# Both feed-forward stages of a two-layer decoder by one level of Strassen

## The reference

```python
def rmsnorm(x, g):
    y = xf * lax.rsqrt(jnp.mean(xf * xf, axis=-1, keepdims=True) + EPS)
    return (y * g.astype(jnp.float32)).astype(x.dtype)

def conv_ffn(h, prev, w_up, conv_w, conv_b, w_down):
    l = h.shape[1]
    u = h @ w_up                                   # 1024 -> 2 * 2816
    ext = jnp.concatenate([prev, u], axis=1)
    y = conv_b + sum(conv_w[k] * ext[:, k:k + l] for k in range(CONV_WIDTH))
    a, v = jnp.split(y, 2, axis=-1)
    return (jax.nn.silu(a) * v) @ w_down, ext[:, -(CONV_WIDTH - 1):]
```

## Time and profile before

| | |
|---|---|
| median of 3 runs | 3037.19 us (3033.56 to 3038.42) |
| span of the profiled execution | 3038.0 us |
| PE busy | 2935.1 us, 97% of the span |
| PEld busy | 2715.8 us, 89% |
| DVE busy | 1574.7 us, 52% |
| POOL busy | 966.5 us, 32% |
| ACT busy | 815.3 us, 27% |
| granted clock of TensorE | 9 tenths of full or more in 38 of the 40 slices of the span |

### The profile page before, as it was taken

The page is one execution under the profiler, slowest core; times in us unless marked ns, Lnnn a source line. Parts: engine busy times, 40 slices in busy tenths (PEclk is TensorE's granted clock), DMA queues, the critical chain, the costliest instruction groups (busy, mean ns, idle before and its releaser), DMA issues. The chain is left out here.

```text
span 3038.0 us, 50987 instructions
## 1 busy us (share of the span) xinstructions
PE 2935.1 (97%) x19316; PEld 2715.8 (89%) x19316; DVE 1574.7 (52%) x3486; ACT 815.3 (27%) x1506; POOL 966.5 (32%) x422
## 2 busy tenths in 40 slices
PE   8998989999989999999999999999999999999998
PEld 7996966666767799999999999997999999999998
DVE  6212158888545418744625535495257626436262
ACT  5002037777623304311201111205133202112020
POOL 4430000000000244544444443460435444444443
PEclk9999989999979999999999999999999999999999
DMA  6116740000457311111111111312111111111112
GB/s 186 54 42 227 252 163 2 2 2 2 149 153 228 128 36 60 40 44 49 38 45 49 34 53 37 129 41 115 43 53 42 40 50 45 40 47 41 50 36 91
DMA packets 128683, 222.76 MB, mean 73 GB/s; under 512 B 16118, under 2 KB 92252, under 8 KB 127344
## 3 DMA queue, kind: packets, MB, share of 16 engines
q1 hardware_dynamic: 108548, 201.57, 20.5%
q10 hardware_dynamic: 19980, 19.14, 2.4%
HBM read 202.61 MB, written 22.18 MB: 74 GB/s over the span
## 5 line engine op out<-in xcount | busy, mean ns | idle before, releaser
L382 POOL TENSOR_SCALAR weights_high<-weights_whole 128x1024 fp32r<-128x1024 f32 (+2 forms) x168 | 434.8, 2588 | 1045.8 <-PE banks L417 878.9
L413 PE MATMUL banks<-ffn_in_high,weights_high 128*128 128x364 f32 (+1 forms) x2112 | 467.0, 329 | 9.6 <-DVE ffn_in_low L280 9.6
L415 PE MATMUL banks<-ffn_in_low,weights_high 128*128 128x364 f32 (+1 forms) x2112 | 466.7, 329 | 0.0
L417 PE MATMUL banks<-ffn_in_high,weights_low 128*128 128x364 f32 (+1 forms) x2112 | 465.2, 329 | 0.0
L384 POOL TENSOR_TENSOR weights_low<-weights_whole,weights_high 128x1024 fp32r<-128x1024 f32 (+2 forms) x168 | 375.7, 2236 | 24.7 <-issue 0.2
L2776 DVE SCALAR_TENSOR_TENSOR conv_out<-conv_ext,conv_w,conv_out 128x1024 f32<-128x1024 f32 x176 | 318.7, 1811 | 114.1 <-ACT conv_out L2708 99.7
L413 PEld LDWEIGHTS banks<-ffn_in_high,weights_high 128*128 128x128 f32 x2112 | 366.1, 189 | 11.4 <-issue 11.4
L417 PEld LDWEIGHTS banks<-ffn_in_high,weights_low 128*128 128x128 f32 x2112 | 367.4, 188 | 0.0
L415 PEld LDWEIGHTS banks<-ffn_in_low,weights_high 128*128 128x128 f32 x2112 | 366.9, 189 | 0.0
L2807 DVE TENSOR_TENSOR x<-x,banks 128x728 f32 (+1 forms) x128 | 86.5, 718 | 385.2 <-PE banks L417 385.2
L2708 ACT ACTIVATE conv_out<-conv_ext,conv_b,conv_w 128x1024 f32<-128x1024 f32 (+1 forms) x176 | 138.3, 835 | 536.1 <-DVEq L2767 536.0
(11 more groups left out here) (433 smaller groups left out, 4616.7 us busy)
## 6 DMA issues: line engine op xcount, KB each, us to landing
weights_whole<-in_w_up SPq DMA_DIRECT2D x88, 512.0 KB, 3.5
past_rows<-in_kv_pages SPq DMA_DIRECT2D x160, 128.0 KB, 2.4
z<-in_kv_pages SPq DMA_DIRECT2D x96, 128.0 KB, 2.4
weights_whole<-in_w_down SPq DMA_DIRECT2D x32, 384.0 KB, 3.1
weights_whole<-in_w_down SPq DMA_DIRECT2D x32, 320.0 KB, 2.9
x<-in_cmp_pages ACTq DMA_DIRECT2D x64, 128.0 KB, 5.8
x<-in_cmp_pages SPq DMA_DIRECT2D x64, 128.0 KB, 5.7
cmp_rows<-in_cmp_pages ACTq DMA_DIRECT2D x64, 128.0 KB, 5.7
```

Of the source, the lines that this page charges most:

```text
L382: pool.tensor_scalar(high, whole, 1.0, None, ALU.mult)
L413: pe.matmul(o, wh, high[:, at], start=kk == 0, stop=False)
L415: pe.matmul(o, wh, low[:, at], start=False, stop=False)
L417: last = pe.matmul(o, wl, high[:, at], start=False, stop=kk == len(terms) - 1)
```

## The change

`conv_ffn` is replaced by `feed_forward`. It works in units. In the up half a unit is one hidden chunk (its a tile and its v tile, 22 units), in the down half two output tiles over a part of the hidden chunks (6 parts, PAIRS, of which five hold 4 chunks and one holds 2; 4 units each). In a unit the weights are a 2 x 2 matrix of blocks (two output tiles by two halves of the input chunks), and the tokens another (two halves of the input chunks by two halves of 544 tokens, TH). The Winograd form of Strassen's scheme gets the four result blocks from 7 block products, where eight were done, with sums of blocks ahead of the products and of products behind them. A block product is 4 input chunks (2 or 1 in the down half) x 3 products x 2 cuts of 272 columns.

- **Weights.** POOL makes the four sums of weight blocks (L2804 to L2812) and the seven low parts (L2797), ACT the seven high parts, in a ring of four blocks; SP loads quarters of weights into six places.
- **Tokens.** They are normalised before the first product: squares (ACT and DVE), sums over the partitions by 72 matmuls of one column (L2845), root (ACT), reciprocal (DVE), a diagonal matrix (L3015) that four matmuls spread over the partitions (L2851). DVE and POOL multiply by it, and make the four sums of token blocks and their seven low parts.
- **Between the halves.** The gated tiles (L3094) go to DRAM (`store`), and come back part by part (`stage`), where ACT cuts the high parts, and DVE the low ones (L3099) and the four sums (L3038).
- **Results.** In the up half ACT copies four blocks of banks per unit and DVE adds three (L3064); in the down half DVE adds each of the 7 products of a unit to `x` (L3112). A product may start when the one two places ahead of it has been read out of its banks.
- The convolution's tiles keep their operations, but the norm is gone from them. `project` no longer cuts the first weights of the stage that follows.

```diff
-PARTS = (6, 6, 5, 5)
+TH = TE // 2
+HP = TH // 2
+KH = KC // 2
+BLOCKS = 7
+RING = 4
+QUARTERS = 6
+PAIRS = (2, 2, 2, 2, 2, 1)
-def conv_ffn(k, layer, w, xn, x, following=(), result=None, saved=None):
...
+def feed_forward(k, layer, w, x, space, following=(), next_w=None, result=None, saved=None):
...
+        LAST_BLOCK = (2, 5, 4, 6)
+        BLOCK_PIECE = (0, 1, 0, None, 2, 1, 3)
...
+            def stage(p):
+                if p == 0:
+                    sp.wait_ge(multiplied, BLOCKS * (FC - 1) + 1)
+                    sp.wait_ge(gated_stored, 16 * 4)
+                elif p == 1:
+                    sp.wait_ge(gated_stored, 16 * FC)
+                else:
+                    sp.wait_ge(d_split, BLOCKS * p)
+                n, at = PAIRS[p], starts[p]
+                for half, dst in enumerate(staged[min(p, 1)]):
+                    src = g_dram[at + half * n:at + (half + 1) * n].rearrange("k p t -> p k t")
+            for q in range(1, UNITS):
+                for piece in range(4):
+                    i = 4 * q + piece
+                    if i >= QUARTERS:
+                        q0, p0 = (i - QUARTERS) // 4, (i - QUARTERS) % 4
+                        sp.wait_ge(w_split, BLOCKS * q0 + LAST_BLOCK[p0] + 1)
+                    sp.dma_start(quarter(q, piece), source(q, piece)).then_inc(q_loaded[i % QUARTERS], 16)
+                    if q == FC and piece == 2:
+                        stage(0)
+                if q == FC + 2:
+                    sp.dma_start(k.outs["conv"][layer], tails[:]).then_inc(stored, 16)
+                    stage(1)
+                elif q > FC + 2 and (q - FC) % PER == 0 and part_of(q) + 1 < len(PAIRS):
+                    stage(part_of(q) + 1)
...
+            def lower(q, j):
+                high, low = ring(q, j)
+                pool.wait_ge(w_rounded, BLOCKS * q + j + 1)
+                pool.tensor_tensor(low, block_source(q, j), high.bitcast(F32), ALU.subtract).then_inc(w_split, 1)
+            def sums(q):
+                a11, a12, a21, a22 = (quarter(q, piece) for piece in range(4))
+                s1 = total[:, 0:width(q) * P]
+                wait_quarter(pool, q, 2)
+                wait_quarter(pool, q, 3)
+                pool.tensor_tensor(s1, a21, a22, ALU.add).then_inc(w_summed, 1)
+                lower(q, 0)
+                lower(q, 1)
+                pool.drain()
+                pool.tensor_tensor(a21, a11, a21, ALU.subtract).then_inc(w_summed, 1)
+                pool.drain()
+                pool.tensor_tensor(a11, s1, a11, ALU.subtract).then_inc(w_summed, 1)
+                pool.drain()
+                pool.tensor_tensor(a12, a12, a11, ALU.subtract).then_inc(w_summed, 1)
+            for q in range(UNITS):
+                sums(q)
+                lower(q, 2)
+                lower(q, 3)
+                if q == 0:
+                    pool.wait_ge(gained, KH)
+                    pool.wait_ge(rstd_ready, 1)
+                    n12 = first_half[:, :, TH:TE]
+                    pool.tensor_tensor(n12, n12, over_half(rstd[:, TH:TE]), ALU.mult).then_inc(pool_normed, 1)
+                    high, low = up_block(4)
+                    pool.wait_ge(rounded, len(UP_ORDER))
+                    pool.tensor_tensor(low, up_quadrant(4), high.bitcast(F32), ALU.subtract).then_inc(last_split, 1)
...
+                src = sq_low[:, kk, :] if kk < 6 else sq_high[:, kk - 6, :]
+                for t in range(NTT):
+                    rows = min(P, TE - t * P)
+                    last = pe.matmul(k.ps[0:rows, 3, t:t + 1], src[:, t * P:t * P + rows], ones[:, 0:1],
+                                     start=n == 0 and t == 0, stop=n == KC - 1, skip_group_check=True)
+            last.then_inc(summed, 1)
+            pe.wait_ge(inverted, 1)
+            flat = spread[:, :, :].rearrange("p a n -> p (a n)")
+            for x_ in range(4):
+                last = pe.matmul(k.ps[:, 4 + x_, 0:HP], ones, flat[:, x_ * HP:(x_ + 1) * HP], start=True, stop=True)
+            last.then_inc(spreaded, 1)
+            def product(q, j):
+                n = width(q)
+                pe.wait_ge(w_split, BLOCKS * q + j + 1)
+                which = "ABAEAEA"[j]
+                wait_read(pe, *((q - 2, "C12"), (q - 1, "C21"), (q, "V1"), (q - 1, "C11"), (q, "V2"), (q, "V5"), (q, "C22"))[j])
+                if q == 0:
+                    if j == 4:
+                        pe.wait_ge(last_split, 1)
+                    elif j:
+                        pe.wait_ge(split, UP_ORDER.index(j) + 1)
+                elif q >= FC and (q - FC) % PER == 0:
+                    pe.wait_ge(d_split, BLOCKS * part_of(q) + DOWN_ORDER.index(j) + 1)
+                wh, wl = ring(q, j)
+                high, low = up_block(j) if q < FC else down_block(part_of(q), j)
+                out = bank(q, which)
...
+                    at = slice(kk * P, (kk + 1) * P)
+                    for z, (a, b) in enumerate(((wh, high), (wh, low), (wl, high))):
+                        for piece in range(2):
+                            last = pe.matmul(out[:, piece, :], a[:, at], b[:, kk, piece * HP:(piece + 1) * HP],
+                                             start=first and kk == 0 and z == 0, stop=kk == n - 1 and z == 2,
...
+                if n >= RING:
+                    act.wait_ge(multiplied, n - RING + 1)
+                if j in (0, 1, 6):
+                    wait_quarter(act, q, BLOCK_PIECE[j])
+                else:
+                    act.wait_ge(w_summed, 4 * q + {3: 1, 4: 2, 2: 3, 5: 4}[j])
+                act.activation(ring(q, j)[0], block_source(q, j), ACT.Copy).then_inc(w_rounded, 1)
...
+            for j, after in ((1, 2), (5, 3), (2, 6), (6, 7), (3, 7), (4, 7)):
+                act.wait_ge(made, after)
+                if j in (3, 4):
+                    act.wait_ge(split, UP_ORDER.index(6) + 1)
+                act.activation(up_block(j)[0], up_quadrant(j), ACT.Copy).then_inc(rounded, 1)
...
+                        last_quadrant(q)
+                    round_weights(BLOCKS * q + j + RING)
+                    if j == 0 and q:
+                        silu(q - 1)
+                    elif j == 2 and q:
+                        store(q - 1)
+                    elif j == 5:
+                        tap(q, 0)
+                    elif j == 6:
+                        tap(q, 1)
+                    if q == FC - 1:
+                        if j == 4:
+                            for block_ in (0, 1, 5):
+                                round_gated(0, block_)
+                        elif j == 6:
+                            for block_ in (2, 3, 4, 6):
+                                round_gated(0, block_)
+                    if p == 0 and i == 7:
+                        silu(FC - 1)
+                    if p == 0 and i == 13:
+                        store(FC - 1)
+                    if p + 1 < len(PAIRS):
+                        for block_, at in zip(DOWN_ORDER, (19, 20, 21, 24, 25, 26, 27) if p == 0 else (8, 9, 10, 15, 16, 17, 18)):
+                            if i == at:
...
+            norm(0)
+            norm(1)
+            lower(0)
+            norm(5)
+            lower(1)
+            dve.wait_ge(pool_normed, 1)
+            difference(n11, n12, n11, made)
+            difference(n12, n22, n12, made)
+            lower(5)
+            difference(n22, n22, n11, made)
+            difference(n21, n21, n22, made)
+            for j in (2, 6, 3):
+                lower(j)
+            dve.wait_ge(last_split, 1)
...
+                tile, half, which = ((0, 0, "A"), (0, 0, "B"), (0, 1, "A"), (1, 1, "E"), (1, 1, "A"), (0, 1, "E"), (1, 0, "A"))[j]
...
+                dve.tensor_tensor(xv, xv, bank(q, which), ALU.add).then_inc(x_added, 1)
+            for q in range(FC):
+                place(q, "C11")
+                place(q, "C22")
+                if q == FC - 1:
+                    lower_gated(0, 0)
+                    lower_gated(0, 1)
+                place(q, "C12")
+                if q == FC - 1:
+                    lower_gated(0, 5)
+                    for j in (3, 4, 2, 6):
+                        gated_sum(0, j)
+                    edges(q, 0)
+                    edges(q, 1)
+                else:
+                    for av in range(2):
+                        edges(q, av)
+                        convolve(q, av, 1)
+                        convolve(q, av, 0)
+                    gate(q)
+            for p in range(len(PAIRS)):
+                for i in range(PER * BLOCKS):
+                    if p == 0 and i in (2, 3, 4, 6):
+                        lower_gated(0, i)
+                    add(FC + p * PER + i // BLOCKS, i % BLOCKS)
+                    if p == 0 and i in (3, 5, 7, 9):
+                        convolve(FC - 1, i // 7, 1 if i in (3, 7) else 0)
+                    if p == 0 and i == 11:
+                        gate(FC - 1)
+                    if p + 1 < len(PAIRS):
+                        late = p == 0
```

(9 more changed lines are left out.)

525 lines of the change are left out of this document (319 added, 206 removed).

## The result

The changed kernel takes 3188.1 us (3186.9 to 3189.8, four runs) against 3036.9, a ratio of 1.0504 [1.0489, 1.0519]: slower by 151 us, where I forecast 75. The profiled execution spans 3187.8 us against 3038.0, 149.8 more; the second stage takes 873.5 of it (2305.52 to 3179.05), 75.3 more than before, the first 69.0 more. The rest is 5.4 us between the stages, 2.0 behind the last, and 1.8 gained ahead of the first.

The account below looks back on a forecast made before the run. It took TensorE's matmul count times spacing as the bound. Matmuls -92.3, start +49, up half +6, between halves +24, staging +20, later parts +29, ends +2 made +37.7 us a stage, +75 in both: 3112 us, range 3010 to 3215.

Parts of the forecast that it names:

- Matmuls: TensorE, both halves: 5544 matmuls of 272 columns at 125.5 ns, 92.3 us less in each stage.
- Rivals 3 and 4: Skill's matmul rule holds at 272 columns, 3004 us, chance 0.04; weight loads bound matmuls at 150 ns, 3384 us, 0.01.
- 72 one-column products ... so they end at some 18 us: Stage start: the sums of squares end at 18 us and the norm at 25, within a start term of +49 us.
- Up half: +6 us: Up half: VectorE and GpSimd taking turns cost 0.3 us for each of 21 units, bounds 0 and 44 us.
- Rival 2: Up half: VectorE's and GpSimd's turns bound it, 23.2 us a unit, 3188 us in all; chance 0.2.
- Rival 1: Turns cost nothing and VectorE is never late at additions: 2987 us, or 3010 at half effect; chance 0.21.
- Turns: VectorE operations on SBUF alone and GpSimd tensor-tensor operations take turns; VectorE operations with an operand in the banks do not.
- Between the halves: +24: Between up and down half: TensorE waits for VectorE's queued work and GpSimd's turns, +24 us a stage, from below 17.
- Staging +20: First down part: fetching gated tiles back from DRAM and VectorE's preparing operations cost +20 us a stage.
- later parts +29: Later down parts: VectorE's additions and preparing operations in one queue cost +29 us a stage, from below 19.
- Ends: +2 a stage: Stage end: next projection's weights cut only after the last unit, last two output tiles leave together, +2 us.
- three signs of being wrong: Up unit over 22.5 us, no down-half gaps at VectorE's additions, or convolution operations beside GpSimd staying at 1.3 us.

Follow-up runs that it names:

- e2: Changed kernel with ScalarE making the up half's last tap before the weight rounding that waits for GpSimd's third sum: 3166.5 us.
- e9: Changed kernel with the tap as in e2, a result addition put before the gate, and ScalarE's store issued after the copy of V5: 3144.8 us.
- e4: Changed kernel with GpSimd's weight sums and low parts cut to 128 columns from each stage's second unit on (work left out): 3102.3 us.
- e5: Changed kernel with the start's sums of squares made by 32 products with a matrix of ones, replacing one-column products and diagonal: 3146.0 us.
- e3: Changed kernel with VectorE making low parts for down products 3, 4 and 6 one addition earlier between the halves: 3158.1 us.
- e7: As e3, with the preparation of the next down part spread out among VectorE's additions: 3153.9 us.
- e11: Changed kernel with e5's start, e9's up half, and eight plain block products per down unit in place of seven: 3003.9 us.

## Why the prediction was wrong in size

- **Matmuls: right.** 125.4 ns from the rows at 256 and 363 columns. The rule columns / 2.4 + 2.5 (the Trainium skill, TensorE: Matmul & The Clock Gate, Back-to-back issue gap), which that section gives for a matmul by itself and not for a stream with weight loads, would be 115.8; the trace differs. Rivals 3 and 4 are out.
- **"72 one-column products ... so they end at some 18 us": the step that failed at the start.** 144 records were taken at 0.129 us, from a row at full clock. In the changed kernel they ran at 0.50 and 0.211 us, 12 us more, the four products with ones took the 4 us of half clock and not 2, and all that follows waits for them: the norm came at 39 us, not 25. The row of before at 18.17 us showed the price at half clock. The chain behind the norm was sized rightly (45 us); but product 2 started only at 79.6 us, behind the copy of V1, so the fifth product came 3 us after that chain's end. Together +16 of 40 us a stage.
- **"Up half: +6 us": mis-sized, +20.** I weighed the engines' loads against the unit (12.6 + 14.3 us) and laid out VectorE alone. What ran over was a chain through ScalarE's queue: GpSimd's third sum, a rounding, the tap, the convolution, the gate, the store, the copy of V5, product 5. e2 takes the first wait out and e9 the last; the load of GpSimd and VectorE is the same there. Rival 2 gave 3188 us, the time that was measured, by luck, and is out all the same: its unit of 23.2 us was 22.0, and is 21.05 in e9 with the same load. Rival 1 is out too: the losses were there in every term, and with less of GpSimd's work beside VectorE 86 us of them go (e4), though how much of that is turns alone no run tells.
- **Turns: right, with one reading off.** The operation of the earlier trace rows at 2709.47 us ends 1.08 us after GpSimd's (2712.52 and 2711.44), not 1.28. In e2 and e5 VectorE's operation ends 1.15 and 2.3 us after GpSimd's, again a little under its own length (1.29 and 2.42).
- **Between the halves: +24, measured 29.** Right in size, but for another reason: 12 us are TensorE and VectorE waiting for each other in turns (e3), not VectorE's amount of work. The wait before the third down product was 7.8 us, not 12.
- **Staging +20 right, later parts +29 four short** (20.4 and 33.3). That VectorE's additions and preparing operations share one queue was the reason given; the rows of e7 and the run e4 add GpSimd's sums, for which ScalarE's queue waits. Plain products need no sums and less of every engine, and have no holes (e11).
- **Ends: +2 a stage, measured 7.4 in both.** The first product of the next projection waits 9.6 us for its low part.

The sum fell short by 40 us a stage: 16 start, 14 up half, 5 between, 4 later parts. All four had the right sign, and each was taken in the lower half of its own bounds. None of the three signs of being wrong came: the up unit stayed under 22.5 us, the down half has gaps at VectorE's additions, and convolution operations beside GpSimd take over 1.3 us.
